# Prompt attention: the projection jobs of the next pair of heads in steps 3 to 12 instead of 0 to 9

## The chip, the cores and the metric

The kernel runs on one core of one Trainium2 chip. The metric is the device time of one execution in microseconds. TensorE (PE) multiplies, VectorE (DVE) and ScalarE (ACT) do elementwise work and move results out of the accumulators (PSUM), SyncE (SP) issues DMAs.

## What is computed

One inference step of a decoder with two layers: the first mixes tokens with multi-head latent attention, the second with causal pooling, and each ends with a gated convolutional FFN. There are 1024 prompt tokens and 8 sequences of 8 sample tokens. The change is in the attention over the prompt, 16 heads, causal:

```
q_lat = jnp.einsum('bthn,khn->bthk', q[..., :QK_NOPE], w_uk)
...
s = (jnp.einsum('bqhk,bsk->bhqs', qb, ckv)
     + jnp.einsum('bqhr,bsr->bhqs', qrb, kr)).astype(jnp.float32) * ATTN_SCALE
s = jnp.where(key_pos[None, :] <= qpos[:, None], s, -jnp.inf)
p = jax.nn.softmax(s, axis=-1).astype(ckv.dtype)
return jnp.einsum('bhqs,bsk->bqhk', p, ckv)
...
o = jnp.einsum('bthk,khv->bthv', o_lat, w_uv).reshape(B, T, N_HEADS * V_HEAD)
```

`ckv` is the compressed latent (256 wide) and `kr` the shared rotated key. The kernel does not attend in the latent space for the prompt: it projects keys and values of each head from `ckv` with `w_uk` and `w_uv`, which gives the same result.

## The kernel before

The program is a row of stages, each a block in which the five engines run their own instruction lists and meet through semaphores: conditioning, projections of the latents, prompt attention (`mla_prompt_stage`), sample attention, output projection, FFN, pooling, FFN. Only the prompt attention is touched.

It works on eight pairs of heads. A pair has sixteen steps (`STEPS = 2 * QB`): step n is query block b = n // 2 (128 queries) of head n % 2, over b + 1 blocks of 128 keys, so the steps grow from 128 to 1024 key columns. For each step there is

- a score on PE (`score`, L1076), into one of two PSUM areas by the step's parity,
- DVE's mask and negated row maximum (`maxes`, L968 and L971),
- ACT's exponential with its row sum (`exps`, L907),
- DVE's reciprocal and scaling (`normalise`, L978 and L980),
- PE's transposes of the probabilities (`turn`, L1092),
- their copy to SBUF, ACT the first four blocks (`first_half`, L914), DVE the rest if there are more than four (`second_half`, L989),
- once per two steps, after the odd one, the product with the values for both heads (`values`, L1107), and after four of these DVE's copy of the result (`attended`, L997).

The engines run these at different distances ahead. In step n PE issues the score of step n + 2, then a job if there is one, in even steps the values product of steps n - 2 and n - 1, and then the transposes of step n. ACT does `first_half` of n - 1 and `exps` of n + 1. DVE does `maxes` of n + 1, `normalise` of n, `attended` of n - 2 and `second_half` of n - 1. After these each takes its part of the job. The values product that belongs to steps 14 and 15 of a pair thus lies in step 0 of the next; the trace shows it as L1107 x32, since the trace counts two matmuls for one instruction in fp32.

While one pair is attended, ten jobs project the next pair's operands. Each is a group of matmuls into one bank (`job_bank`), which is copied out by ACT (k and v jobs, L896 and L898) or DVE (q jobs, L959 and L961), and the next job waits until that is done:

```
JOBS = [("k", 0), ("k", 1), ("v", 0), *Q_JOBS[0:2], ("v", 1), *Q_JOBS[2:]]
SLOT_OF_JOB = dict(zip(range(10), range(len(JOBS))))
```

A k job projects 512 keys (L1052), a v job four blocks of values (L1060), a q job one of three token chunks of one head, with weights and activations in two fp32r parts, so in three matmuls (L1045 to L1047). The texts call the jobs k0, k1, v0, q00, q01, v1, q02, q10, q11, q12 in their order. The q jobs need the weights' parts: in step 0 ACT rounds the next pair's weights (`split`, wq_hi, L885), and DVE takes the remainder (wq_lo, L949) ahead of all its other work of that step. Job k0 waits for wq_hi, too. SP loads the weights of a pair (L838) once all jobs of the pair two before are done.

`SLOT_OF_JOB` gives the steps in which jobs stand, and ACT, DVE and PE all follow it:

```
if n in SLOT_OF_JOB and not last:
    job(i + 1, SLOT_OF_JOB[n], 1 - s)
```

Pair 0's own jobs are done before its first step, and pair 7 has no next pair, so it has no jobs. Pair 0 and pair 7 are written out, the six between are a loop of two pairs.

Of the kernel before, what the change touches and what calls it, by code (L numbers as in the profile page):

```python
# [783 lines left out]
def mla_prompt_stage(k, m):  # L784
# [4 lines left out]
    with ExitStack() as own:  # L789
# [30 lines left out]

        Q_JOBS = [("q", hh, c) for hh in range(2) for c in range(NC)]
        JOBS = [("k", 0), ("k", 1), ("v", 0), *Q_JOBS[0:2], ("v", 1), *Q_JOBS[2:]]
        SLOT_OF_JOB = dict(zip(range(10), range(len(JOBS))))
        BY_DVE = [kind == "q" for kind, *_ in JOBS]
        BY_ACT = [kind != "q" for kind, *_ in JOBS]
        FIRST_Q = JOBS.index(Q_JOBS[0])
# [25 lines left out]
        def at(i, n, ahead):  # L852

            over, m = divmod(n + ahead, STEPS)
            return STEPS * i + n + ahead, i + over, m
# [22 lines left out]
        def _(act):  # L878
# [8 lines left out]
            def job(i, j, s):  # L887
                if not BY_ACT[j]:
                    return
                kind, half = JOBS[j]  # L890
                bank = bank_of_job(i, j)
                act.wait_ge(job_done, 10 * i + j + 1)
                if kind == "k":
                    for hh in range(2):
                        r = slice(64 * hh, 64 * hh + 64)
                        last = act.activation(keys[s][r, hh, half * 512:(half + 1) * 512], bank[r, :], ACT.Copy)  # L896
                else:
                    last = act.activation(vals[s][:, half * 4:half * 4 + 4, :],  # L898
                                          bank.rearrange("p (j n) -> p j n", n=P), ACT.Copy)
                last.then_inc(job_a, 1)  # L900
# [15 lines left out]
            def pair(i, s, turn, first=False, last=False):  # L916
                hi, exp = (each_step(i, first, last, *x) for x in ((-1, first_half), (1, exps)))
                for n in range(STEPS):
# [3 lines left out]
                    exp(n)  # L922
                    if n in SLOT_OF_JOB and not last:
                        job(i + 1, SLOT_OF_JOB[n], 1 - s)

# [13 lines left out]
        def _(dve):  # L939
# [11 lines left out]
            def job(i, j, s):  # L951
                if not BY_DVE[j]:
                    return
                _, hh, c = JOBS[j]
                t0, w = prompt_cols(c)
                bank = bank_of_job(i, j)
                dve.wait_ge(job_done, 10 * i + j + 1)
                if c == NC - 1:
                    dve.tensor_tensor(m.qs[:, bass.ds(2 * i + hh, 1), :], bank[:, w:w + NS].unsqueeze(1),  # L959
                                      rot[:, hh, SEQ:NT].unsqueeze(1), ALU.mult).then_inc(samples_q, 1)  # L960
                dve.tensor_tensor(q[s][:, hh, t0:t0 + w], bank[:, 0:w], rot[:, hh, t0:t0 + w], ALU.mult)\  # L961
                   .then_inc(job_d, 1)
# [37 lines left out]
            def pair(i, s, first=False, last=False):  # L1000
                most, norm, take, lo = (each_step(i, first, last, *x) for x in
                                        ((1, maxes), (0, normalise), (-2, attended), (-1, second_half)))
                for n in range(STEPS):
# [5 lines left out]
                    lo(n)  # L1009
                    if n in SLOT_OF_JOB and not last:  # L1010
                        job(i + 1, SLOT_OF_JOB[n], 1 - s)

# [13 lines left out]
        def _(pe):  # L1026
# [37 lines left out]
            def score(N, i, n, s):  # L1064

                b, hh = divmod(n, 2)
                out = scores[n % 2]
                if n == 0:
                    d, a = job_counts(i + 1, 0)
                    pe.wait_ge(job_a, a)  # L1070
                    pe.wait_ge(job_d, d)
                wait(pe, exp_done, N - 1)
                w = n_blocks(n) * P
                for o in range(0, w, 512):
                    e = min(o + 512, w)
                    last = pe.matmul(out[:, o:e], q[s][:, hh, b * P:(b + 1) * P], keys[s][:, hh, o:e],  # L1076
                                     start=True, stop=True)
                last.then_inc(s_done, 1)
# [32 lines left out]
            def pair(i, s, first=False, last=False):  # L1111
                for n in range(STEPS):
                    if not (last and n + 2 >= STEPS):
                        score(*at(i, n, 2), s if n + 2 < STEPS else 1 - s)
                    if n in SLOT_OF_JOB and not last:
                        job(i + 1, SLOT_OF_JOB[n], 1 - s)
                    if n % 2 == 0 and not (first and n == 0):
# [329 lines left out]
def mla(k):  # L1447
    with ExitStack() as own:
        m = Latents(k, own)
        with ExitStack() as latent:  # L1450
            m.cq_hi = k.sbuf(latent, "cq_hi", [P, QT, NT], F32R)
            m.cq_lo = k.sbuf(latent, "cq_lo", [P, QT, NT], F32R)
            mla_project_stage(k, m)
            k.stage_done()
            mla_prompt_stage(k, m)
            k.stage_done()
        mla_sample_stage(k, m)
        k.stage_done()
        mla_out_stage(k, m)
        k.stage_done()  # L1460
# [670 lines left out]
```

## Time and profile before

| what | us |
|---|---|
| median of 3 runs | 2976.69 (2976.57 to 2980.84) |
| the profiled execution, its own time | 2976.89 |
| its span, first to last instruction | 2975.1 |
| PE busy | 2696.2 (91%) |
| DVE busy | 1772.6 (60%) |
| ACT busy | 1028.8 (35%) |

The span is one execution on the core; the time of the execution includes 1.8 us around it. The prompt attention with its jobs begins at about 331 us and ends at 828 us. Starts in the timeline count from the span's start. Matmuls are pipelined, so a group's duration overlaps the next group's start a little; the distance between two starts is the better measure of what a group takes. PEclk is the granted clock of TensorE as a share of its full 2.4 GHz: it is either 1.00 or 0.50, and values between are a stretch's mean over both.

### The profile page before, as it was taken

What the parts mean: (1) busy time and instruction counts of PE and PEld (TensorE: products, weight loads), DVE (VectorE), ACT (ScalarE), POOL (GpSimd) and SP (SyncE); (2) the same over time, 40 slices, a digit from 0 to 9 for tenths busy, and PEclk for the clock granted to TensorE, in tenths of its full rate; (3) what the DMA queues carried; (4) which work ended last, traced back from release to release, by engine and by line L of the source; (5) the groups of instructions that cost most, each with busy time, mean ns of one, the idle gap of its engine ahead of it and who ended that gap; (6) DMA issues with size and microseconds to landing.
All of it is one profiled execution on the core that took longest, in us unless ns stands there. A gap on an engine that the chain in (4) does not pass through costs nothing. (4 is left out here: it accounts for less than half of the span.)

```text
span 2975.1 us, 43092 instructions
## 1 busy us (share of the span) xinstructions
PE 2696.2 (91%) x15678; PEld 2321.5 (78%) x15678; DVE 1772.6 (60%) x3116; ACT 1028.8 (35%) x1692; POOL 99.8 (3%) x71
## 2 busy tenths in 40 slices
PE   6979699889978988999999999867799999999996
PEld 2558466666656958999999999723599999999993
DVE  3961355555623146666666666665666666666665
ACT  4842243434413144333333333233433333333322
POOL 0000000000000020000000000042100000000001
PEclk8989899999989999999999999988899999999998
DMA  7920100000063210111111111000111111111101
GB/s 295 413 75 32 48 12 22 11 25 0 1 209 107 103 36 29 43 43 51 50 47 42 42 42 42 13 29 0 43 47 51 50 43 42 42 42 42 42 28 66
DMA packets 42730, 178.48 MB, mean 60 GB/s; under 512 B 6146, under 2 KB 9730, under 8 KB 38690
## 3 DMA queue, kind: packets, MB, share of 16 engines
q1 hardware_dynamic: 41938, 176.81, 16.5%
q8 instruction: 45, 0.74, 0.1%
q10 hardware_dynamic: 720, 0.71, 0.1%
q14 instruction: 27, 0.22, 0.0%
HBM read 170.43 MB, written 7.07 MB: 60 GB/s over the span
## 5 line engine op out<-in xcount | busy, mean ns | idle before, releaser
L1857 DVE TENSOR_TENSOR ffn_y<-psum,ffn_y 128x384 f32<-128x384 f32 (+1 forms) x1056 | 554.7, 534 | 495.7 <-PE psum L1917 495.1
L1915 PE MATMUL psum<-ffn_h_hi,ffn_w_hi 128*128 128x384 f32 (+1 forms) x2112 | 692.9, 328 | 18.3 <-DVE ffn_h_lo L431 18.3
L1916 PE MATMUL psum<-ffn_h_lo,ffn_w_hi 128*128 128x384 f32 (+1 forms) x2112 | 695.4, 329 | 0.0
L1917 PE MATMUL psum<-ffn_h_hi,ffn_w_lo 128*128 128x384 f32 (+1 forms) x2112 | 692.1, 328 | 0.0
L1915 PEld LDWEIGHTS psum<-ffn_h_hi,ffn_w_hi 128*128 128x128 f32 x2112 | 399.1, 189 | 19.0 <-DVE ffn_h_lo L431 18.9
L1917 PEld LDWEIGHTS psum<-ffn_h_hi,ffn_w_lo 128*128 128x128 f32 x2112 | 399.4, 189 | 0.0
L1916 PEld LDWEIGHTS psum<-ffn_h_lo,ffn_w_hi 128*128 128x128 f32 x2112 | 399.0, 189 | 0.0
L1915 PE MATMUL psum<-ffn_g_hi,ffn_w_hi 128*128 128x384 f32 (+1 forms) x1056 | 357.6, 339 | 19.5 <-DVE ffn_g_lo L1878 15.1
L1916 PE MATMUL psum<-ffn_g_lo,ffn_w_hi 128*128 128x384 f32 (+1 forms) x1056 | 346.8, 328 | 0.0
L1917 PE MATMUL psum<-ffn_g_hi,ffn_w_lo 128*128 128x384 f32 (+1 forms) x1056 | 346.5, 328 | 0.0
L1767 ACT ACTIVATE ffn_u<-psum 128x384 f32<-128x384 f32 (+1 forms) x264 | 119.7, 454 | 548.4 <-PE psum L1917 442.8
L1915 PEld LDWEIGHTS psum<-ffn_g_hi,ffn_w_hi 128*128 128x128 f32 x1056 | 199.2, 189 | 52.9 <-DVE ffn_y L1857 28.7
L1826 DVE SCALAR_TENSOR_TENSOR ffn_work<-ffn_u,ffn_taps,ffn_work 128x1024 f32<-128x1024 f32 x176 | 225.4, 1281 | 16.0 <-ACT ffn_work L1770 13.5
L1916 PEld LDWEIGHTS psum<-ffn_g_lo,ffn_w_hi 128*128 128x128 f32 x1056 | 199.6, 189 | 0.0
L1917 PEld LDWEIGHTS psum<-ffn_g_hi,ffn_w_lo 128*128 128x128 f32 x1056 | 199.4, 189 | 0.0
L1770 ACT ACTIVATE ffn_work<-psum,ffn_taps 128x384 f32<-128x384 f32 (+1 forms) x264 | 172.9, 655 | 0.0
L1794 ACT ACTIVATE ffn_work<-ffn_work 128x1088 f32<-128x1088 f32 x44 | 49.0, 1114 | 351.1 <-DVE ffn_work L1830 351.1
L1814 DVE TENSOR_TENSOR ffn_w_lo<-ffn_raw,ffn_w_hi 128x1024 fp32r<-128x1024 f32 x132 | 157.5, 1219 | 20.6 <-ACT ffn_w_hi L1753 20.3
L1753 ACT ACTIVATE ffn_w_hi<-ffn_raw 128x1024 fp32r<-128x1024 f32 x132 | 135.6, 1065 | 49.5 <-DMA ffn_raw<-in_ffn_w 47.3
L1076 PE MATMUL psum<-keys,q 128*128 128x512 f32 (+3 forms) x384 | 146.2, 490 | 2.1 <-ACT prob L907 1.3
L914 ACT ACTIVATE prob_t<-psum 128x512 f32<-128x512 f32 (+3 forms) x128 | 66.2, 517 | 215.0 <-PE psum L1092 214.5
L337 DVE TENSOR_TENSOR ada_w_lo<-ada_w,ada_w_hi 128x2048 fp32r<-128x2048 f32 x48 | 107.7, 2287 | 23.1 <-ACT ada_w_hi L271 22.8
(230 smaller groups left out, 3637.1 us busy)
## 6 DMA issues: line engine op xcount, KB each, us to landing
ffn_raw<-in_ffn_w SPq DMA_DIRECT2D x132, 512.0 KB, 5.1
ada_w<-in_ada_w SPq DMA_DIRECT2D x24, 2048.0 KB, 10.7
cache<-in_cache SPq DMA_DIRECT2D x64, 320.0 KB, 4.9
x<-in_x SPq DMA_DIRECT2D x2, 4352.0 KB, 17.8
pair_raw<-in_pair_w SPq DMA_DIRECT2D x8, 768.0 KB, 4.4
wo_raw<-in_wo SPq DMA_DIRECT2D x8, 512.0 KB, 4.0
proj_raw<-in_proj_w SPq DMA_DIRECT2D x7, 512.0 KB, 3.8
out_x_out<-x SPq DMA_DIRECT2D x2, 1536.0 KB, 6.0
```

The source lines that it names most:

```text
L337: dve.tensor_tensor(w_lo[:, s % 2, cols], w[:, s, cols], w_hi[:, s % 2, cols], ALU.subtract)\
L914: act.activation(prob_t[s][:, 0:w], turn_bank[:, o:o + w], ACT.Copy).then_inc(turned_a, 1)
L1076: last = pe.matmul(out[:, o:e], q[s][:, hh, b * P:(b + 1) * P], keys[s][:, hh, o:e], start=True, stop=True)
L1753: act.activation(w_hi[s][:], raw[s][:], ACT.Copy).then_inc(hi_ready[s], 1)
L1767: act.activation(u[s][:, 2 + t0:2 + t0 + w], bank[:, 0:w], ACT.Copy)
L1770: act.activation(conv[s][:, t0:t0 + n_], bank[:, 0:n_], ACT.Identity, bias=bias, scale=tap2)\
L1814: dve.tensor_tensor(w_lo[s][:], raw[s][:], w_hi[s][:], ALU.subtract).then_inc(lo_ready[s], 1)
L1826: dve.scalar_tensor_tensor(cp, u[s][:, tap:tap + SEQ], taps[:, bass.ds(m, 1), tap], cp, ALU.mult, ALU.add).then_inc(conv_step[s], 1)
L1857: dve.tensor_tensor(dst, down_bank[i % 2][:, 0:n_], dst, ALU.add).then_inc(acc_done, 1)
L1915: pe.matmul(bank[:, a], w_hi[s][:, w], act_hi, start=first, stop=False)
L1916: pe.matmul(bank[:, a], w_hi[s][:, w], act_lo, start=False, stop=False)
L1917: return pe.matmul(bank[:, a], w_lo[s][:, w], act_hi, start=False, stop=last)
```

## The change

The ten jobs stand in steps 3 to 12 of the pair before, in the same order, where they stood in steps 0 to 9. Steps 0, 1 and 2 have no job any more, steps 10, 11 and 12 have one. Each job's evacuation on ACT or DVE moves with it. The splitting of the weights stays in step 0.

```
         JOBS = [("k", 0), ("k", 1), ("v", 0), *Q_JOBS[0:2], ("v", 1), *Q_JOBS[2:]]
-        SLOT_OF_JOB = dict(zip(range(10), range(len(JOBS))))
+        SLOT_OF_JOB = dict(zip(range(3, 13), range(len(JOBS))))
         BY_DVE = [kind == "q" for kind, *_ in JOBS]
```

In PE's list, the boundary of two pairs in the loop, from the transposes of step 15 on, stood like this before:

```order
L1092 MATMUL psum<-ident,prob 128x128 x8
L867 ISA
L1076 MATMUL psum<-keys,q 128x256
L1033 REGISTER_ALU
L1052 MATMUL psum<-ckv,pair_raw 128x512 x2
L1101 REGISTER_ALU
L1107 MATMUL psum<-prob_t,vals 64x128 x16
L867 REGISTER_ALU
L1092 MATMUL psum<-ident,prob 128x128
```

and stands like this now:

```order
L1092 MATMUL psum<-ident,prob 128x128 x8
L867 ISA
L1076 MATMUL psum<-keys,q 128x256
L1101 REGISTER_ALU
L1107 MATMUL psum<-prob_t,vals 64x128 x16
L867 REGISTER_ALU
L1092 MATMUL psum<-ident,prob 128x128
L867 REGISTER_ALU
L1076 MATMUL psum<-keys,q 128x256
```

k0 (L1052) no longer stands between the first score of the new pair and the product with the values of step 15 (L1107).

Steps 9 and 10 on PE, from the transposes of step 9 on, before:

```order
L1092 MATMUL psum<-ident,prob 128x128 x5
L867 REGISTER_ALU
L1076 MATMUL psum<-keys,q 128x512
L1076 MATMUL psum<-keys,q 128x384
L1101 REGISTER_ALU
L867 REGISTER_ALU
L1107 MATMUL psum<-prob_t,vals 64x128 x10
L1092 MATMUL psum<-ident,prob 128x128 x6
```

and now (the job's later matmuls, three times the same three, are left out at the end):

```order
L1092 MATMUL psum<-ident,prob 128x128 x5
L867 REGISTER_ALU
L1076 MATMUL psum<-keys,q 128x512
L1076 MATMUL psum<-keys,q 128x384
L867 REGISTER_ALU
L1045 MATMUL psum<-cq_hi,wq_hi 128x384
L1046 MATMUL psum<-cq_lo,wq_hi 128x384
L1047 MATMUL psum<-cq_hi,wq_lo 128x384
L1045 MATMUL psum<-cq_hi,wq_hi 128x384
```

Job q10 follows the score of step 10, ahead of the product with the values.

DVE's list in steps 10 and 11 of pair 0, the difference:

```order
 L980 TENSOR_SCALAR prob<-prob,softmax_stats 128x768
 L989 COPY prob_t<-psum 128x256
+L961 TENSOR_TENSOR q<-psum,rot 128x384
 L968 TENSOR_TENSOR psum<-psum,mask 128x128
 L971 TENSOR_REDUCE softmax_stats<-psum 128x1
```

The evacuation of job q10 (L961) now stands ahead of the next step's mask and maximum.

## Rows read from the trace of the kernel before

**Rows 1.** The profile page, busy time of each engine: us, share of the span, instructions.

```profile
PE 2696.2 (91%) x15678; PEld 2321.5 (78%) x15678; DVE 1772.6 (60%) x3116; ACT 1028.8 (35%) x1692; POOL 99.8 (3%) x71
```

**Rows 2.** Windows, prompt attention: length, busy of five engines, clock, DMA share, GB/s.

```profile
352.00:830.00 478.00, 425.91 (x2907) 316.78 (x2908) 273.88 (x657) 194.54 (x433) 0.00 (x0) 0.97 0.04 13
```

**Rows 3.** Waits of PE in that stretch: us in total, times, longest us.

```profile
PE psum L1107 <- DVE prob_t L989: 29.8, 30, 2.3
```

**Rows 4.** PE's timeline, pair 5's step 14 to pair 6's step 0: start, length, [idle before].

```profile
715.92 2.98 PE L1107 MATMUL psum<-prob_t,vals 128*64 128x128 f32 x28 [1.99 <-DVE prob_t L989]
...
722.19 0.60 PE L1076 MATMUL psum<-keys,q 128*128 128x256 f32 x2
723.98 1.98 PE L1052 MATMUL psum<-ckv,pair_raw 128*128 128x512 f32 x4 [1.20 <-ACT wq_hi L885]
726.77 1.97 PE L1107 MATMUL psum<-prob_t,vals 128*64 128x128 f32 x32 [0.80 <-DVE prob_t L989]
```

**Rows 5.** Timeline of ACT and DVE around the same boundary.

```profile
722.88 1.05 ACT L885 ACTIVATE wq_hi<-pair_raw 128x1024 fp32r<-128x1024 f32 x1
723.96 1.23 DVE L949 TENSOR_TENSOR wq_lo<-pair_raw,wq_hi 128x1024 fp32r<-128x1024 f32 x1 [2.84 <-ACT wq_hi L885]
...
726.03 0.68 DVE L989 COPY prob_t<-psum 128x512 f32<-128x512 f32 x1
```

**Rows 6.** PE's timeline, steps 1 to 3 of pair 6.

```profile
729.26 1.88 PE L1052 MATMUL psum<-ckv,pair_raw 128*128 128x512 f32 x4
730.98 0.27 PE L1092 MATMUL psum<-ident,prob 128*128 128x128 f32 x1
...
732.43 2.05 PE L1060 MATMUL psum<-pair_raw,ckv 128*128 128x128 f32 x16 [0.53 <-ACT keys L896]
...
735.05 0.81 PE L1076 MATMUL psum<-keys,q 128*128 128x384 f32 x2
```

**Rows 7.** PE's timeline, score and v job in step 5 of pair 6.

```profile
742.02 1.02 PE L1076 MATMUL psum<-keys,q 128*128 128x512 f32 x2
742.88 1.95 PE L1060 MATMUL psum<-pair_raw,ckv 128*128 128x128 f32 x16
```

**Rows 8.** PE's timeline, steps 0 to 3 of pair 7, which has no jobs.

```profile
784.83 1.97 PE L1107 MATMUL psum<-prob_t,vals 128*64 128x128 f32 x32 [0.44 <-DVE prob_t L989]
...
789.37 0.81 PE L1076 MATMUL psum<-keys,q 128*128 128x384 f32 x2
```

**Rows 9.** PE's timeline, pair 0's step 14, then steps 10, 12 and 14 of pair 6.

```profile
408.05 2.33 PE L1107 MATMUL psum<-prob_t,vals 128*64 128x128 f32 x28 [2.08 <-DVE prob_t L989]
...
764.12 1.31 PE L1107 MATMUL psum<-prob_t,vals 128*64 128x128 f32 x20 [0.91 <-DVE prob_t L989]
...
770.39 1.53 PE L1107 MATMUL psum<-prob_t,vals 128*64 128x128 f32 x24 [0.27 <-DVE prob_t L989]
...
777.53 3.13 PE L1107 MATMUL psum<-prob_t,vals 128*64 128x128 f32 x28 [1.99 <-DVE prob_t L989]
780.59 1.33 PE L1092 MATMUL psum<-ident,prob 128*128 128x128 f32 x8
```

**Rows 10.** Windows of the granted clock, columns as in rows 2.

```profile
716.30:719.60 3.30, 3.30 (x30) 2.97 (x27) 0.92 (x3) 0.00 (x0) 0.00 (x0) 0.50 0.00 0
722.80:726.80 4.00, 2.02 (x6) 0.71 (x6) 2.77 (x7) 2.16 (x6) 0.00 (x0) 1.00 0.00 0
856.30:863.00 6.70, 4.94 (x13) 2.94 (x14) 1.64 (x3) 1.30 (x4) 0.00 (x0) 0.50 0.83 298
...
409.00:409.50 0.50, 0.50 (x10) 0.50 (x8) 0.29 (x1) 0.00 (x0) 0.00 (x0) 0.56 0.06 16
...
777.50:778.00 0.50, 0.47 (x6) 0.47 (x8) 0.47 (x3) 0.00 (x0) 0.00 (x0) 0.70 0.00 0
```

**Rows 11.** PE's timeline, transposes in the sample attention.

```profile
857.92 1.97 PE L1317 MATMUL psum<-ident,sprob 128*128 128x128 f32 x8 [4.06 <-DVE sprob L1263]
...
872.23 1.09 PE L1317 MATMUL psum<-ident,sprob 128*128 128x128 f32 x8
```

## The prediction

> **What bounds the kernel now.** I began with the busy shares: TensorE (PE) works 91% of the span [rows 1], so only what makes PE wait, or slows its clock, matters. The change sits in the prompt attention, 478 us of the span, where PE is busy 425.91 us at a mean granted clock of 0.97 [rows 2]. The waits of that stretch come next: the largest for PE is the product with the values (L1107) for a DVE copy of the turned probabilities, 29.8 us in 30 waits [rows 3]. The timeline then shows where they lie, and each of the seven pairs with jobs repeats them:
>
> - Between steps 1 and 9 a job stands in every step and PE hardly waits: 0.53 us in step 2 [rows 6].
> - Steps 10 and 12, without a job, wait 0.91 and 0.27 us for that copy [rows 9], and step 14 waits 1.99 us [rows 4].
> - At the boundary of two pairs PE's last score before step 0's job starts at 722.19 and ends at 722.79; job k0 follows at 723.98, the product of step 15 at 726.77 [rows 4]. That product waits for a chain on the other engines, which k0 has no part in: ACT rounds the next pair's weights (722.88), DVE takes the remainder (723.96), then a step's softmax work, then the copy (726.03 to 726.71) [rows 5].
>
> The clock is the second thing. Behind the idle stretch of step 14 it is at 0.50, so at 1.2 GHz instead of 2.4, from 716.3 to 719.6 [rows 10]. A mean of 0.97 over 478 us is 0.03 / 0.5 x 478 = 29 us at the low level, nine such stretches: one in step 14 of each of the eight pairs, where L1107 x28 takes 2.3 us or more all eight times (the shortest in [rows 9]), and one ahead of pair 0's step 0.
>
> **The change part by part**, for one of the pairs 1 to 6 (pair 7 has no jobs in either kernel).
>
> *Jobs k1 and v0 leave steps 1 and 2.* From the product of step 15 to the score issued in step 3 takes 735.05 - 726.77 = 8.28 us with them [rows 4, 6]. Pair 7 does the same work without them in 789.37 - 784.83 = 4.54 us [rows 8]. -3.74 us.
>
> *Job k0 leaves step 0.* It lay inside the chain of ACT and DVE. That chain stays: without k0 the product still starts 4.0 us after the last score. Gain 0.
>
> *Ten jobs stand in steps 3 to 12, where seven stood in 3 to 9.* The added work is that of two k jobs and one v job. A k job is 730.98 - 729.26 = 1.72 us [rows 6]; a v job is busy 1.95 us [rows 7], of which 0.16 overlaps what follows, as with the k job (1.88 against 1.72), so 1.79. Together +5.23 us.
>
> *The new jobs in steps 10 and 12 cover waits.* 2 us of matmuls hide the 0.91 and 0.27 us. -1.18 us. Step 14's wait is untouched: it starts from the end of the last score, and steps 13 to 15 get no job.
>
> *The jobs' evacuations move too.* ACT's copy of k0 must be out of the one job bank before k1. From k1's end to v0's start that took 732.43 - 730.98 = 1.45 us [rows 6]. Between k0 and k1 now lie a score of 512 columns, 742.88 - 742.02 = 0.86 us [rows 7], and two transposes, a quarter of the 1.09 us of eight [rows 11], 0.24 us. A new wait of 0.35 us. On DVE the q evacuations of steps 10 to 12 stand ahead of the next maximum. I cost them at 0: PE has a product (1.31 us [rows 9]), transposes (0.8) and a score (twice the 0.86 above), 3.8 us, before it needs what is queued there; if that cover failed each of the three steps would wait like step 10 does now, 0.91 us. SP's load of a pair's weights waits for the jobs of the pair two before, three steps later than now, and has over a pair's length left. 0.
>
> Sum of the schedule: -3.74 + 5.23 - 1.18 + 0.35 = +0.66 us a pair, +4.0 us for six. In pair 0 there is no product of a step 15 to wait for; part of k0's time comes back there and the low clock stretches what follows. I take 0, between -1 and +1.
>
> *The clock.* Without k0, PE idles 4.0 us at each boundary; now it is busy 2.02 of these 4.00 us and the clock stays at 1.00 [rows 10]. The nearest row for such a gap is in the sample attention: PE idles 4.06 us, and the next eight transposes take 1.97 us where later ones take 1.09 [rows 11], with the clock at 0.50 from 856.3 to 863.0 [rows 10]. So I expect a new fall at each of six boundaries. Its price: at most half of the low time behind the gap, (863.0 - 857.9) / 2 = 2.5 us; at least 0. A fall in step 14 costs 1.6 us: the product with 28 matmuls takes 3.13 where 24 take 1.53 and 32 take 1.97, so about 1.75, and the eight transposes 1.33 against 1.09 [rows 4, 9, 11]. I take 1.7, near the price in this stage. 6 x 1.7 = +10.2 us.
>
> Against that, some falls of step 14 may go. They are not tied to an instruction: in pair 0 the clock falls about 1 us after the product starts (408.05; the slice at 409.0 has 0.56), in pair 6 about 0.2 us after (777.53; the slice at 777.5 has 0.70) [rows 9, 10]. The fall slips against the work by 0.14 us a pair, and boundaries that are over 2 us longer move it much further, so that I expect it to miss part of the pairs. Bounds are none and all eight; I take the middle, four: -6.5 us.
>
> The Trainium skill (TensorE: Matmul & The Clock Gate, "Why this matters for your kernels") warns against long idle gaps between bursts of matmuls; taken at its word the 4 us gap is paid for and nothing is given back, which is the first rival below, whereas the rows show the clock down after 1.99 us of idleness already. The same page ("What's actually happening") says that the gate's count runs freely and does not start with the kernel; the slip above agrees.
>
> Total: 4.0 + 0 + 10.2 - 6.5 = +7.7 us on the profiled execution's 2976.89 us: 2984.6. The median of the runs is 0.2 us lower, so **2984.4 us**, 0.26% slower. A measurement can tell about 0.2%, 6 us, from no change.
>
> **The rivals.**
>
> 1. The step 14 falls all stay: +4.0 + 10.2 = +14.2, 2990.9 us. For it: the idle 1.99 us are unchanged. Against: the slip. Chance 0.17.
> 2. The clock holds across the boundary, and step 14 is as before: +4.0, 2980.7 us. For: 2.02 us of work spread otherwise was enough. Against: the sample attention's gap. 0.15.
> 3. Faster: the clock stays up in step 14, since the jobs in steps 10 to 12 keep PE busy right before it, and no boundary falls. -8 x 1.6 + 4.0 = -8.8, 2967.9 us. It decides once over six of the eight falls are gone without new ones (4.0 + 6 = 10 us against 1.6 each). Against: PE was busy before step 14 already, without gaps but 0.27 us. 0.07.
> 4. DVE becomes the bound of steps 10 to 12, with 0.91 us in each: 3 x 0.91 x 6 = 16.4 more than the forecast, 3000.8 us; half of it 2992.6. For: a q evacuation blocks the next maximum until PE is done. Against: 3.8 us of cover. 0.08.
>
> That the change does nothing is out: the order of PE's instructions shows the jobs moved.
>
> **How the numbers follow.** The forecast has 0.53. Its own spread is from 4 us (four falls gone, a cheap new fall) to 12; about a quarter of it lies under 6 us. Slower by over 0.2%: 0.40 of the forecast, rivals 1 and 4: 0.64. Same: 0.12 of the forecast, rival 2 and part of 3: 0.29. Faster: 0.07. The range from 2979 to 2993 leaves out rival 3 and the far ends of 1 and 4.
>
> **What would show it.** Right: in pairs 1 to 6 an idle stretch of about 4 us before L1107 x32, no wait of 0.91 in step 10, the score of step 3 some 4.5 us after that product's start at full clock, clock 0.50 behind each boundary, and L1107 x28 near 1.75 us in about half of the pairs. Wrong: a clock of 1.00 behind the boundaries, all eight slow L1107 x28, or waits for DVE ahead of the transposes of steps 10 to 12.

## The result, and the profile after

The changed kernel takes 2982.24 us in the median of 12 runs (2978.43 to 2987.51), the kernel before 2975.37 us in 12 runs (2971.55 to 2980.84). The ratio is 1.0023 with a 95% interval of 1.0014 to 1.0032: slower by 6.9 us, between 4 and 10. The prediction said 0.26% and 7.7 us. The spans of the two profiled executions differ by 2980.7 - 2975.1 = 5.6 us.

Busy time on the profile page after, to [rows 1]:

```profile
PE 2698.9 (91%) x15678; PEld 2326.5 (78%) x15678; DVE 1773.4 (59%) x3116; ACT 1028.0 (34%) x1692; POOL 99.8 (3%) x71
```

All engines are busy for as long as before, within 3 us, and the weight loads (PEld) within 5. The work is the same, so the answer is in waits and clock. Windows of the changed kernel, columns as in [rows 2]; the first is the prompt attention, the second lies behind the boundary of pairs 3 and 4, the third in front of it:

```profile
353.50:833.00 479.50, 425.29 (x2876) 317.21 (x2878) 273.61 (x654) 194.32 (x433) 0.00 (x0) 0.96 0.04 13
608.30:611.60 3.30, 3.30 (x26) 2.53 (x21) 0.85 (x2) 0.69 (x3) 0.00 (x0) 0.50 0.00 0
603.40:607.40 4.00, 0.07 (x1) 0.00 (x0) 2.69 (x7) 1.67 (x4) 0.00 (x0) 1.00 0.00 0
```

The stage's mean clock went from 0.97 to 0.96. In the last 4.0 us ahead of the values product PE is busy 0.07 us, where it was busy 2.02 us [rows 10]; 0.8 us into the product the clock falls to 0.50, so to 1.2 GHz. PE's waits there (us in total, times, longest), to [rows 3]:

```profile
PE psum L1107 <- DVE prob_t L989: 42.1, 17, 4.1
...
PE psum L1052 <- ACT keys L896: 1.4, 7, 0.2
```

29.8 us in 30 waits became 42.1 us in 17, the longest 4.1 us. The waits of 0.91 and 0.27 us are gone, those at the boundary grew. PE's timeline from pair 3's step 14 to pair 4's step 4, to [rows 4, 6]:

```profile
598.22 1.75 PE L1107 MATMUL psum<-prob_t,vals 128*64 128x128 f32 x28 [1.99 <-DVE prob_t L989]
...
602.87 0.60 PE L1076 MATMUL psum<-keys,q 128*128 128x256 f32 x2
607.45 2.94 PE L1107 MATMUL psum<-prob_t,vals 128*64 128x128 f32 x32 [3.98 <-DVE prob_t L989]
...
613.23 0.81 PE L1076 MATMUL psum<-keys,q 128*128 128x384 f32 x2
...
615.60 0.38 PE L1092 MATMUL psum<-ident,prob 128*128 128x128 f32 x2
615.82 1.02 PE L1076 MATMUL psum<-keys,q 128*128 128x512 f32 x2
617.04 1.99 PE L1052 MATMUL psum<-ckv,pair_raw 128*128 128x512 f32 x4 [0.20 <-ACT keys L896]
```

From above: 1.99 us idle in step 14 as before, but this time the product of 28 matmuls runs at full clock (1.75 us). The last score starts at 602.87 and ends at about 603.47; the product of step 15 follows 4.0 us later, with nothing between. It takes 2.94 us, not 1.97, at the low clock. The score of step 3 starts 5.78 us after it. Between k0 and k1 is a wait of 0.20 us for ACT's copy of the keys. Steps 10 and 12 of pair 4, to [rows 9], have no idle time left:

```profile
643.18 1.31 PE L1107 MATMUL psum<-prob_t,vals 128*64 128x128 f32 x20
...
652.97 1.53 PE L1107 MATMUL psum<-prob_t,vals 128*64 128x128 f32 x24
```

### The profile page after: what moved, and what is told of

Its sections match the earlier page's. It is cut to its first block and busy times, and to the rows that moved or that the text cites. A ratio compares the mean times of both kernels' runs of the same rounds, so it can differ in the third digit from the quotient of the medians.

```text
span 2980.7 us, 43092 instructions
## 1 busy us (share of the span) xinstructions
PE 2698.9 (91%) x15678; PEld 2326.5 (78%) x15678; DVE 1773.4 (59%) x3116; ACT 1028.0 (34%) x1692; POOL 99.8 (3%) x71
## 5 line engine op out<-in xcount | busy, mean ns | idle before, releaser
L1076 PE MATMUL psum<-keys,q 128*128 128x512 f32 (+3 forms) x384 | 149.8, 500 | 3.4 <-ACT prob L907 2.6
L1107 PE MATMUL psum<-prob_t,vals 128*64 128x128 f32 x1152 | 86.3, 300 | 42.3 <-DVE prob_t L989 42.1
```

The source lines that it names most:

```text
L1107: last = pe.matmul(o_bank[r, b % 4 * P:(b % 4 + 1) * P], vals[s][:, kb, r], prob_t[hh][:, kb * P:(kb + 1) * P], start=kb == 0, stop=kb == b)
```

## The experiments

All times are medians, and ratios are to the kernel before measured on the same chip. For each trace I also took the prompt attention alone, from its first score (L1076) to the first matmul of the sample attention (L1285, or the same statement some lines lower), and counted the falls of the clock in slices of 0.5 us. "Late splitting" stands for the changed kernel with the splitting of the weights moved out of step 0:

| kernel | first score | end | stage, us | falls in step 14 | falls at boundaries |
|---|---|---|---|---|---|
| before | 352.34 | 829.42 | 477.08 | 8 | 0 |
| changed | 353.50 | 835.94 | 482.44 | 4 | 6 |
| changed, boundaries filled | 352.92 | 829.92 | 477.00 | 5 | 0 |
| changed, k0 stays in step 0 | 354.16 | 818.21 | 464.05 | 4 | 0 |
| changed, late splitting | 353.14 | 807.66 | 454.52 | 4 | 0 |
| before, step 14 filled | 352.25 | 816.90 | 464.65 | 0 | 0 |
| changed, both filled | 351.81 | 820.82 | 469.01 | 0 | 0 |
| before, last three jobs moved | 353.06 | 820.82 | 467.76 | 5 | 0 |
| late splitting, v1 in step 13 | 353.67 | 791.49 | 437.82 | 1 | 0 |
| late splitting, q12 in step 13 | 354.46 | 809.36 | 454.90 | 3 | 0 |
| before, second profile | 353.43 | 827.75 | 474.32 | 6 | 0 |
| changed, second profile | 353.82 | 834.92 | 481.10 | 2 | 6 |
| boundaries filled, second profile | 353.94 | 832.45 | 478.51 | 5 | 0 |

Pair 7's boundary with pair 6 has no splitting and counts as none. Two kinds of low stretch are in neither column. One lies at pair 0's step 0 in every trace, 3.4 us long in some and 6.8 in others; it hardly matters, since from the first score to pair 0's product of step 14 the kernel before takes 55.7 us and the changed one 55.8. The other lies at pair 7's product of step 15, in four traces: late splitting, last three jobs moved, and the second profiles of the kernel before and of the filled boundaries. There that product takes 3.31 to 3.68 us instead of 1.97. Where a fill is used, it is a few matmuls into the idle job bank whose result nobody reads.

### The boundaries filled

```
+                    if n == 0 and not (first or last):
+                        for _ in range(3):
+                            pe.matmul(job_bank, k.ident[:], m.ckv[:, 0, 0:512], start=True, stop=True)
                     if n in SLOT_OF_JOB and not last:
```

> The changed kernel, with three matmuls of 512 columns (about 2.6 us) whose result nobody reads, issued in step 0 of pairs 1 to 6 between the first score and the product with the values of step 15, inside the 4.0 us in which PE idles. Clock theory: the idle stretch shrinks to about 1.4 us and the product still starts at the same distance from the last score, so the schedule is untouched, but the clock stays at 1.00 behind all six boundaries and L1107 x32 takes 1.97 us there. That gives back about 1.7 us six times, 10 us; some of the four step 14 falls that had gone return, since the pairs get shorter again (1.6 us each), so 6 to 10 us under the changed kernel, 2972 to 2976, about level with the kernel before. Rival, the schedule alone (jobs moved out of a shadow): the idle PE time is what costs, filling it with useless work changes nothing, 2982.

2980.47 us, ratio 1.002 (1.001 to 1.003). The timeline shows the product of step 14 of pair 2 and that of step 15 behind it:

```profile
533.30 1.75 PE L1107 MATMUL psum<-prob_t,vals 128*64 128x128 f32 x28 [1.99 <-DVE prob_t L989]
...
542.61 1.97 PE L1107 MATMUL psum<-prob_t,vals 128*64 128x128 f32 x32 [1.49 <-DVE prob_t L989]
```

PE idles 1.49 us instead of 4.0, the product starts when it did, and it takes 1.97 us at full clock. All six boundary falls are gone, one more step 14 fall is there, and the stage is 5.4 us shorter. The falls and the product's length came as expected. The time did not: the median of the whole program is only 1.8 us under the changed kernel's, where I expected 6 to 10. The nine times lie in two groups, two at 2973.6 to 2973.9 us, the profiled execution among them, and seven at 2978.1 to 2982.5, which the last three runs take up.

### Job k0 stays in step 0

```
-        SLOT_OF_JOB = dict(zip(range(3, 13), range(len(JOBS))))
+        SLOT_OF_JOB = dict(zip([0, *range(4, 13)], range(len(JOBS))))
```

> The changed kernel with job k0 back in step 0 and the other nine jobs in steps 4 to 12. Clock and shadow theory: k0 costs nothing in step 0 (the product of step 15 starts 4.0 us after the last score with or without it), so each of pairs 1 to 6 has one job less in steps 3 to 12 than the changed kernel, -1.7 us, loses its 0.2 to 0.35 us wait for the keys copy, and keeps the clock at the boundary, -1.7 us; against the kernel before it is -3.74 + 1.72 + 1.79 - 1.18 = -1.4 us a pair, -8.5 us, and 0 to 4 of the eight step 14 falls gone: 2961 to 2968. Rival, that the new place of the jobs in steps 10 to 12 costs as such (DVE's queue): not faster than before, 2975 or more.

2965.36 us, ratio 0.9973 (0.9963 to 0.9983). As expected. The product of pair 3's step 14, then k0 and the product of step 15:

```profile
587.80 1.75 PE L1107 MATMUL psum<-prob_t,vals 128*64 128x128 f32 x28 [1.99 <-DVE prob_t L989]
...
594.24 1.98 PE L1052 MATMUL psum<-ckv,pair_raw 128*128 128x512 f32 x4 [1.20 <-ACT wq_hi L885]
597.02 1.97 PE L1107 MATMUL psum<-prob_t,vals 128*64 128x128 f32 x32 [0.80 <-DVE prob_t L989]
```

k0 stands inside the wait as in [rows 4], with the same 1.20 and 0.80 us around it, and costs nothing there. Moving the other nine jobs is a gain of 10 us, so it is k0 alone that turns the change into a loss. Apart from the clock, k0's new place costs about its own length, 1.7 us: from one product of step 14 to the next, a pair in which no fall lies takes 59.0 us here and 60.7 to 60.8 us in the changed kernel with both fills (below). The schedule's gain is smaller than I wrote, though: before, such a pair takes 60.0 to 60.1 us (with step 14 filled, below), so 1.0 us a pair and not 1.4.

### The splitting leaves step 0

```
                     hi(n)
-                    if n == 0 and not last:
-                        split(i + 1, 1 - s, turn)
                     exp(n)
+                    if n == 2 and not last:
+                        split(i + 1, 1 - s, turn)
...
-                    if n == 0 and not last:
-                        split(i + 1, 1 - s)
                     most(n)
...
                     lo(n)
+                    if n == 3 and not last:
+                        split(i + 1, 1 - s)
```

> The changed kernel with the splitting of the next pair's weights taken out of step 0: ACT rounds in step 2 behind its exponential, DVE takes the remainder in step 3 behind its step work; the jobs stay in steps 3 to 12. If the 4.0 us idle stretch is the chain ACT rounding - DVE remainder - softmax - DVE copy, it falls to the 0.44 us that pair 7 shows, in six pairs: -3.5 us each, -21 us, and the boundary falls of the clock go with it, -10 us, while one or two more step 14 falls may return (1.6 us each) : 2950 to 2958. If the copy was late for another reason (the transposes of step 15, or DVE's general load) the wait stays over 2 us and the time over 2970.

2953.09 us, ratio 0.9929 (0.9916 to 0.9943), in the range. Products of step 14 of pair 3 and of step 15:

```profile
581.25 1.75 PE L1107 MATMUL psum<-prob_t,vals 128*64 128x128 f32 x28 [1.99 <-DVE prob_t L989]
...
586.84 1.97 PE L1107 MATMUL psum<-prob_t,vals 128*64 128x128 f32 x32 [0.35 <-DVE prob_t L989]
```

The wait at the boundary is 0.35 us instead of 4.0. So the 4 us were the chain of ACT's rounding and DVE's remainder and not the transposes or a general load of DVE. The changed slots are what allows this: with k0 in step 3 nothing asks for the split weights in step 0.

### Step 14 filled in the kernel before

```
+                    if n == 14:
+                        for _ in range(2):
+                            pe.matmul(job_bank, k.ident[:], m.ckv[:, 0, 0:512], start=True, stop=True)
```

> The kernel before, with two matmuls of 512 columns (about 1.7 us) whose result nobody reads, issued in step 14 of every pair between the score and the product with the values, inside the 1.99 us of idleness. Clock theory: the clock stays at 1.00 in step 14 of all eight pairs, L1107 x28 takes 1.75 us instead of up to 3.2, and the schedule is otherwise the same: 8 x 1.6 = 13 us faster, 2962. Rival, the low clock there costs little because DVE and ACT are waited for anyway: within 4 us of the kernel before. A third outcome: the fill delays the product and the time rises by up to 8 x 0.3 us.

2966.47 us, ratio 0.9972 (0.9962 to 0.9981). The products of step 14 and step 15 of pair 2:

```profile
528.03 1.75 PE L1107 MATMUL psum<-prob_t,vals 128*64 128x128 f32 x28 [0.27 <-DVE prob_t L989]
...
537.34 1.97 PE L1107 MATMUL psum<-prob_t,vals 128*64 128x128 f32 x32 [0.63 <-DVE prob_t L989]
```

The wait shrinks to 0.27 us, the product takes 1.75 us, and no pair has its fall. In the stage this is 477.08 - 464.65 = 12.4 us for eight falls, 1.55 each, as expected. The medians of the whole program differ by 9 us, 4 less than I wrote; the two profiled executions differ by 12.1. That useless work makes the kernel faster, with the product at 1.75 us in all eight pairs, shows that the clock costs time there.

### Both filled in the changed kernel

The two fills above together.

> The changed kernel with both fills of matmuls that nobody reads: three in step 0 of pairs 1 to 6, two in step 14 of every pair. No fall of the clock should be left in either place, as in the kernel before with its step 14 filled (2966.5), so the two compare the bare schedules. By the prediction's terms the changed schedule is 0.66 us a pair slower (0.5 with the wait for the keys copy of 0.2 us that its trace shows), 3 to 4 us: 2969 to 2971, and no L1107 x28 or x32 over 2.0 us. Rival, the whole difference of the two kernels (6.9 us) lies in the schedule and the clock terms cancel otherwise: 2973 or more. Rival, it lies in the clock alone: 2966.

2968.20 us, ratio 0.9982 (0.9973 to 0.9991). The intervals of this kernel and of the kernel before with step 14 filled overlap, so the runs alone do not separate them; the stage does, 469.01 against 464.65 us, neither with a fall. The bare schedule is 4.4 us slower (predicted 4.0). From pair 0's product of step 14 to pair 6's it is 364.49 against 360.19 us, so 0.72 us a pair where 0.66 was predicted. The product of step 15 at the start of pair 4, pair 4's score of step 3, and its k1:

```profile
599.10 1.97 PE L1107 MATMUL psum<-prob_t,vals 128*64 128x128 f32 x32 [1.41 <-DVE prob_t L989]
...
603.72 0.81 PE L1076 MATMUL psum<-keys,q 128*128 128x384 f32 x2
...
607.53 1.98 PE L1052 MATMUL psum<-ckv,pair_raw 128*128 128x512 f32 x4 [0.21 <-ACT keys L896]
```

4.62 us from the product to the score (predicted 4.54, from pair 7), and 0.21 us for the keys copy (predicted 0.35).

### Only the last three jobs moved

```
-        SLOT_OF_JOB = dict(zip(range(10), range(len(JOBS))))
+        SLOT_OF_JOB = dict(zip([*range(7), 10, 11, 12], range(len(JOBS))))
```

> The kernel before with only its last three jobs (q10, q11, q12) moved from steps 7 to 9 to steps 10 to 12; jobs stand in steps 0 to 6. By the prediction's terms they cover the waits of 0.91 and 0.27 us in seven pairs, -8.3 us, at no cost in steps 7 to 9 (pair 7 has no wait there without jobs either), k0 stays in the shadow, and with pairs 1.2 us shorter part of the eight step 14 falls go (none to five, 1.6 us each): 2959 to 2968. Rival, DVE's queue: a q evacuation ahead of the maximum in the long steps delays the transposes: waits of PE for DVE in steps 10 to 12, and no gain, 2973 or more.

2965.29 us, ratio 0.9964 (0.9950 to 0.9977), in the range. PE's waits for DVE's copies:

```profile
PE psum L1107 <- DVE prob_t L989: 22.2, 17, 2.3
...
PE psum L1092 <- DVE prob_t L989: 5.6, 8, 0.9
```

The first was 29.8 us in 30 waits [rows 3]: 7.6 us less, close to the 8.3 us of seven pairs. The second, ahead of the transposes, did not grow (5.5 us before), so DVE's queue in steps 10 to 12 is no bound. Three of eight falls in step 14 are gone as well. The stage gained 9.3 us, less than 7.6 plus three falls: in this trace the low stretch of pair 7's step 14 goes on for 10.2 us, where the kernel before has 3.4.

### v1 in step 13

The late splitting, and:

```
-        JOBS = [("k", 0), ("k", 1), ("v", 0), *Q_JOBS[0:2], ("v", 1), *Q_JOBS[2:]]
-        SLOT_OF_JOB = dict(zip(range(3, 13), range(len(JOBS))))
+        JOBS = [("k", 0), ("k", 1), ("v", 0), *Q_JOBS, ("v", 1)]
+        SLOT_OF_JOB = dict(zip(range(4, 14), range(len(JOBS))))
```

> A version meant to beat all: the late splitting of the weights (2953.1) with the ten jobs in steps 4 to 13 and v1 put last, so that the job in step 13 is evacuated by ACT. It lies ahead of the 1.99 us wait of step 14, which starts from the end of the last score, so PE works 1.8 us of it: -1.99 us in seven pairs, -14 us, and no step 14 fall of the clock in those pairs (three of them left in the late splitting's trace, 1.6 us each, -5 us): 2932 to 2940. If ACT's copy of v1 delays its copy of the turned probabilities or the next exponential, the gain is smaller: up to 0.6 us a pair, 2944.

2938.33 us, ratio 0.9878 (0.9863 to 0.9893): the fastest of all, 37 us under the kernel before. Step 13 and the product of step 14 of pair 3:

```profile
568.38 1.88 PE L1076 MATMUL psum<-keys,q 128*128 128x512 f32 x4
570.10 1.95 PE L1060 MATMUL psum<-pair_raw,ckv 128*128 128x128 f32 x16
571.88 0.93 PE L1092 MATMUL psum<-ident,prob 128*128 128x128 f32 x7
...
573.57 1.75 PE L1107 MATMUL psum<-prob_t,vals 128*64 128x128 f32 x28 [0.18 <-ACT prob_t L914]
```

The v job (L1060) lies between the last score and the transposes, DVE does its step meanwhile, and the product waits 0.18 us instead of 1.99. Only pair 7, which has no job, still has its fall.

### q12 in step 13

As before this, but with `JOBS` in its old order.

> As the version with v1 last, but with the jobs in their old order, so that q12 stands in step 13. Its evacuation is DVE's, queued ahead of step 14's maximum, scaling and copy, so DVE starts those only once the job is done: the wait of step 14 stays near 2 us (1.9 us of job, then 0.6 + 2.8 us of DVE against 1.2 us of PE's transposes and score), the falls of the clock too, and the time is that of the late splitting alone, 2950 to 2957. If DVE's order did not matter, it would be as fast as with v1 last.

2955.25 us, ratio 0.9933 (0.9919 to 0.9946). The score of step 15, the transposes of step 13 after the q job, and the product of step 14:

```profile
578.16 1.88 PE L1076 MATMUL psum<-keys,q 128*128 128x512 f32 x4
...
581.64 0.92 PE L1092 MATMUL psum<-ident,prob 128*128 128x128 f32 x7
...
585.36 1.75 PE L1107 MATMUL psum<-prob_t,vals 128*64 128x128 f32 x28 [2.23 <-DVE prob_t L989]
```

The wait of 2 us is back in full, though a job stands in the same step. A q job is emptied by DVE, ahead of its work for the next step in its queue. The trace shows DVE waiting for the job's last matmul (L1047) and only then starting on the mask, though the score that it masks began at 578.16:

```profile
581.96 0.23 DVE L959 TENSOR_TENSOR qs<-psum,rot 128x64 f32 x1 [2.69 <-PE psum L1047]
...
582.43 0.29 DVE L968 TENSOR_TENSOR psum<-psum,mask 128x128 f32<-128x128 f32 x1
```

So it is the engine that empties the job's bank that decides. The time came out as I wrote. Of the falls in step 14 three are left, against four in the late splitting's trace; whether the longer work ahead of the wait has a part in that is not shown.

### Second profiles

The kernels before, changed, and changed with filled boundaries, each once more, unedited.

> The changed kernel, unchanged, for a second profile. All six boundaries fall again, since they idle 4.0 us wherever the phase lies, and three to five of the eight step 14 falls, not always in the same pairs as in the first profile (pairs 0, 2, 6 and 7).

> The changed kernel with its boundaries filled, unchanged from the first experiment, for a second profile. Its eleven or so times lay in two groups, two at 2973.6 to 2973.9 (the first profile, with five step 14 falls, among them) and seven at 2978.1 to 2982.5. If the number of step 14 falls is what separates them, a profile whose own time is in the upper group has seven or eight of them in the prompt attention (1.6 us each: 3 more are 5 us). If it has five as well, the difference lies in another stage.

Both counts of step 14 falls missed my ranges by one: six before (seven or eight expected), two after (three to five). The boundary falls came six times of six, as expected. The reason that I gave for the first range does not hold in this trace: its pairs with a fall last 61.3 to 61.4 us and not 61.5 to 61.6, the fall comes 1.1 to 1.3 us after the product's start, a little later from pair to pair, and pairs 5 and 6 have none. The third has five falls in step 14 as in its first profile, and yet takes 2983.37 us against 2973.59. So most of the difference lies in another stage. The span and the mean granted clock of the first and of the second profile:

```profile
core 0: 2971.8 us, clock 0.961
```

```profile
core 0: 2981.6 us, clock 0.957
```

9.8 us apart in the span; 1.0 is there at the first score, the stage adds 1.5 (the low stretch at pair 7's last product, 3.42 us instead of 1.97), and the other 7.3 us come after it. Of these, 4.1 us arise right ahead of the FFN's first product, in a stretch that takes 50.1 us at a mean clock of 0.89 instead of 46.0 us at 0.96, and 2.4 us in the 889 us that follow. The mean clock of 0.961 against 0.957 is 0.004 / 0.5 x 2980 = 24 us more at the low level over the whole program, which can cost up to half of that.

## Why the prediction was right

The forecast was slower by 7.7 us; 6.9 was measured. The mechanism was right. That the two numbers are so close is luck in part: the prompt attention itself got 5.4 us longer in the first pair of profiles and 6.8 in the second (481.10 - 474.32), with different counts of falls. The parts, from the first traces of the prompt attention:

| term | predicted | measured |
|---|---|---|
| bare schedule, all pairs | +4.0 | +4.4 (469.01 - 464.65) |
| new falls at six boundaries | +10.2 | +8.2 |
| step 14 falls that go | -6.5 | -7.2 (what is left over) |
| sum | +7.7 | +5.4 (482.44 - 477.08) |

The third row was not measured by itself. It is what the fills leave over, so that the column adds up by construction.

- **k0 was free in step 0.** Right, and the heart of it. The product of step 15 starts 4.0 us after the last score without k0, as it did with it. The version that leaves k0 in place is 10 us faster than before; in the one that takes the chain away the wait of 4.0 us falls to 0.35.
- **Steps 1 and 2.** -3.74 us predicted; 4.62 instead of 4.54 us makes it -3.66.
- **Steps 10 and 12.** The waits are gone as predicted; moving three jobs alone took 7.6 us of them off in one trace.
- **The keys copy.** A new wait, 0.20 us where I put 0.35. ACT is as quick as I took it to be: from k0's end to k1's start it is 617.04 - 615.60 = 1.44 us, against 1.45. The score and the transposes between them cover 1.24 us of that and not 1.10, since the score's last 0.16 us, which I had left out as overlap, count where nothing follows it at once.
- **The new falls.** Six of six in both traces. Their price was the term sized worst: from the product to the score of step 3 the six boundaries take 6.07, 6.15, 5.72, 5.78, 6.24 and 5.97 us against 4.62 at full clock, in sum 8.2, so 1.37 us each and not 1.7. The stretch is as long as in step 14, 3.4 us, and costs at most half of that, 1.7 us; the short wait for the exponential in step 2, up to 0.37 us at full clock, swallows part of it. In the second profile the six take 9.0 us more than at full clock; at pair 3's end the stretch is 6.8 us long there.
- **The step 14 falls.** Four stayed and four went, the number I had taken as the middle between none and all; in the second profile only two stayed. So the number was luck in part. A faster kernel was out of its reach: with all eight gone the sum would still be 4.4 + 8.2 - 12.4 = +0.2 us, no change. That the falls come and go with the length of the pairs, as the prediction's slip has it, remains an argument; no run changed that length and nothing else. Their worth in the stage follows from the runs with fills: (477.08 - 464.65) before, less what is left of (482.44 - 469.01) after the 8.2 us, 12.4 - 5.2 = 7.2. The four that stayed thus cost 1.3 us each and not 1.6.
- **The rivals.** Not all step 14 falls stay (the first); the clock does not hold at the boundary (the second); nothing is faster (the third); DVE is no bound in steps 10 to 12 (the fourth): PE's waits for it ahead of the transposes are 5.4 us in total, 5.5 before. The prediction's chances by outcome are a hundredth or two off: its slower parts add up to 0.65, not 0.64.
- **From the stage to the program.** The stage accounts for 5.4 of 5.6 us between the two spans once 1.2 us that arose ahead of it and 0.9 us gained after it are set off. The medians differ by 1.3 us more than the spans, within their interval. That single executions have more or fewer falls in other stages, I had not thought of at all.

What stays open: why the version with filled boundaries lies in the upper group in seven of nine runs. The one trace from that group shows the time behind the prompt attention and a lower mean clock, not what sets it off.

## What to carry to other kernels

A job that stood inside somebody else's wait was free here and kept PE's clock up; before moving such a job, look at what the engine does in the place that it leaves, not only at the waits it could cover in the new one. Better still, ask what the wait consists of: here it was another engine's preparation that nothing needed yet, and moving that was worth 29 us where moving the jobs cost 7. And look at who empties a filler job: the one that ACT empties left 0.18 us of the wait, the one that DVE empties, the engine waited for, left 2.23.

## What the runs showed of the hardware

- The granted clock fell to 1.2 GHz in all eight pairs of the first profile behind 1.99 to 2.30 us of idleness of TensorE, between 0.1 us before and 1.0 us after the start of the product that followed, and 1.7 us of useless matmuls inside that time kept it at 2.4 GHz in all eight. The kernel with them is 9 us faster. Where the idle stretch was broken up by k0 into 1.20 and 0.80 us, the clock stayed at 2.4 GHz in all six boundaries.
- The falls are not bound to a place in the program. The same kernel had eight in one execution and six in another, the changed one four and two in step 14. Two executions of one program, 9.8 us apart in their spans, differed by 1.5 us in the stage with the experiment and by 7.3 us behind it. For differences of 0.2% the trace of the stage says more than a few runs of the whole, if its falls are counted: the stage of the kernel before took 477.08 us with eight falls in step 14, and 474.32 with six and one at pair 7's last product.
